# Mixture of experts in the order of their counts: second blocks on loaded weights, 64-row experts in pairs

## What is computed

```
gp = softmax(h @ w_rg + b_rg);  g_top, g_idx = top_k(gp, 1)
e_val, e_idx = top_k(el, 2)                       # two experts of the chosen group
expert = g_idx * 8 + e_idx
...
# expert e on its rows x: (silu(x @ w1[e]) * (x @ w3[e])) @ w2[e]
...
y = sum over the two of weights * y_expert
```

## Time and profile before

| | us |
|---|---|
| median of 3 runs | 2807.04 |
| lowest and highest run | 2804.06, 2811.59 |
| span of the profiled execution | 2805.2 |
| first matmul of the expert products (PE) | 674.40 |
| last matmul of the expert stage | 1250.21 |
| last matmul of the overflow stage | 1315.62 |
| first matmul of the next stage | 1329.25 |

### The profile page before, as it was taken

One profiled execution on the slowest core, in us unless ns is written; L12 is line 12 of the kernel. 1 busy time (PEld: TensorE's weight loads), 2 busy tenths in 40 slices (PEclk: granted clock), 3 DMA queues, 4 the chain that ended last, 5 costly groups with the idle time before them and its releaser, 6 DMA issues. The chain is left out here.

```text
span 2805.2 us, 34722 instructions
## 1 busy us (share of the span) xinstructions
PE 2696.0 (96%) x13265; PEld 2307.2 (82%) x13265; DVE 2087.0 (74%) x2831; ACT 1433.1 (51%) x1907; POOL 933.4 (33%) x493
## 2 busy tenths in 40 slices
PE   7999998996999999997988999999999999999999
PEld 4878886685888888876866899999999988888888
DVE  6376645556988888886664689788888778888883
ACT  4232124424777887766342334578878533333332
POOL 1425441231222222221222346533333434444420
PEclk9999999997999999998889999999999999999999
DMA  7336321115999999997310335689999999999992
GB/s 273 107 129 244 120 90 45 58 50 223 356 370 390 382 365 360 359 343 278 110 53 27 101 104 176 214 304 349 352 346 342 372 355 377 376 376 379 381 354 98
DMA packets 174282, 707.59 MB, mean 252 GB/s; under 512 B 24960, under 2 KB 52384, under 8 KB 140064
## 3 DMA queue, kind: packets, MB, share of 16 engines
q1 hardware_dynamic: 90864, 464.38, 45.2%
q0 software_dynamic: 47232, 142.66, 13.6%
q10 hardware_dynamic: 36016, 98.28, 9.3%
HBM read 661.70 MB, written 72.88 MB: 262 GB/s over the span
## 5 line engine op out<-in xcount | busy, mean ns | idle before, releaser
L2341 ACT ACTIVATE peer_high<-ring 128x1024 fp32r<-128x1024 f32 x268 | 283.1, 1056 | 318.9 <-PE psum L137 318.9
L2473 DVE TENSOR_TENSOR peer_low<-ring,peer_high 128x1024 fp32r<-128x1024 f32 x216 | 264.7, 1225 | 196.3 <-ACT peer_high L2341 191.9
L135 PE MATMUL psum<-h_high,peer_high 128*128 128x384 f32 (+1 forms) x1152 | 398.5, 346 | 3.2 <-DVE h_low L2623 3.2
L137 PE MATMUL psum<-h_high,peer_low 128*128 128x384 f32 (+1 forms) x1152 | 393.0, 341 | 0.0
L136 PE MATMUL psum<-h_low,peer_high 128*128 128x384 f32 (+1 forms) x1152 | 393.0, 341 | 0.0
L129 POOL TENSOR_TENSOR mx_slab_low<-mx_half_slab,mx_slab_high 128x1024 fp32r<-128x1024 f32 x85 | 215.1, 2533 | 397.2 <-ACT mx_slab_high L120 343.6
L1475 DVE TENSOR_TENSOR slab_low_moe<-half_slab_moe,slab_high_moe 128x2048 fp32r<-128x2048 f32 x126 | 285.6, 2288 | 52.0 <-ACT slab_high_moe L1417 51.9
L2226 POOL DMA_INDIRECT pe_rows<-in_v_rows,pe_place x128 | 202.5, 1582 | 251.3 <-DVE pe_sums L2595 215.8
L2226 POOL DMA_INDIRECT pe_rows<-in_u_rows,pe_place x128 | 167.9, 1312 | 282.7 <-DVE pe_row_act L2583 264.3
L1417 ACT ACTIVATE slab_high_moe<-half_slab_moe 128x2048 fp32r<-128x2048 f32 x126 | 234.0, 1908 | 24.9 <-issue 24.9
L135 PE MATMUL psum<-slab_high_moe,moe_x_high 128*128 128x512 f32 x560 | 224.4, 401 | 7.3 <-issue 3.7
(11 more groups left out here) (495 smaller groups left out, 6520.3 us busy)
## 6 DMA issues: line engine op xcount, KB each, us to landing
half_slab_moe<-in_weights SPq DMA_DIRECT2D x128, 1024.0 KB, 8.2
ring<-in_weights SPq DMA_DIRECT2D x162, 512.0 KB, 4.7
hT<-in_weights SPq DMA_DIRECT2D x64, 1024.0 KB
ring<-in_v_rows SPq DMA_DIRECT2D x128, 512.0 KB
mx_half_slab<-in_weights SPq DMA_DIRECT2D x44, 1024.0 KB, 5.1
gates_rows<-pe_table ACTq DMA_DIRECT2D x12, 2048.0 KB
pe_gt<-gates_rows ACTq DMA_DIRECT2D x16, 1536.0 KB
gelu_rows<-pe_gl ACTq DMA_DIRECT2D x30, 768.0 KB
```

What stands on the lines that cost most here:

```text
L135: pe.matmul(out, w[0], x[0], start=start, stop=False)
L137: return pe.matmul(out, w[1], x[0], start=False, stop=stop)
L2341: act.activation(high[:, g % RING, :], raw[:, g % RING, :], ACT.Copy).then_inc(highs, 1)
L2473: dve.tensor_tensor(low[:, g % RING, :], raw[:, g % RING, :], high[:, g % RING, :].bitcast(F32), ALU.subtract).then_inc(lows_dve, 1)
```

## The change

The blocks are laid out by rank. `stage_route` ranks the experts by their counts (expert 0 always comes first, as its first slabs are loaded before the route is known). Ranks 0 to 15 have a block of their own. Ranks 16 to 31 have at most 64 rows each (sixteen others have at least as many, and there are 1024 rows), and rank 16 + i shares a gathered block with rank 24 + i: slots 0 to 63 and 64 to 127. Ranks 1 to 3 get a second block, always. What goes beyond that still goes to the overflow stage, which now has 5 bodies and not 7. So there are 16 + 8 + 3 = 27 gathered blocks and 35 units of products: 13 of kind "whole", 3 "twice", 3 "again" (the second block of a "twice") and 16 "small".

The units run in the order: whole (rank 0), whole (4), small (16), small (24), twice (1), again (1), whole (5), small (17), small (25), twice (2), again (2), and so on. A small unit holds 64 columns of rows on PE and still streams 512 columns of weights. An "again" unit uses the slabs of its "twice" unit: they stay in their places for both, and its gate goes to bank 7, its down to banks 7 and 0. SP now takes the expert's number from `m.steer` for every expert but the first. The overflow stage loses its early start in the expert stage: the first load, gather and split of an overflow block move into `body`, and the last store of the expert stage moves out of it.

```diff
-OVER = 7
-BLOCKS = EXPERTS + OVER + 1
+OVER = 5
+SMALL = 64
+PAIRS = 8
+WHOLE = EXPERTS - 2 * PAIRS
+TWICE = 3
+C_AGAIN = WHOLE + PAIRS
+C_OVER = C_AGAIN + TWICE
+BLOCKS = C_OVER + OVER
...
+            chain(dve.scalar_tensor_tensor(out=key[:, :], in0=count, scalar=float(E), in1=less_number[:, :],
+                                           op0=ALU.mult, op1=ALU.add))
+            chain(dve.tensor_tensor(above[:, :, :], bcast(key[:, :], 1, E), bcast(key[:, :], 2, E), ALU.is_gt))
+            chain(dve.tensor_reduce(place_of[:, :], above[:, :, :], AX.X, ALU.add))
...
+            chain(dve.tensor_tensor(blocks_hot[:, :, :, :], bcast(flat_hot, 1, 4), bcast(blocks_of[:, :, :], 2, 2 * TT), ALU.mult))
+            chain(dve.tensor_reduce(blocks[:, :, :], blocks_hot[:, :, :, :], AX.X, ALU.add))
...
-            chain(dve.tensor_tensor(tmp[:, :, :, :], starts.unsqueeze(1).unsqueeze(1).to_broadcast([P, 2, TT, E]),
-                                    hot[:, :, :, :], ALU.mult))
-            chain(dve.tensor_reduce(ov[:, :, :], tmp[:, :, :, :], AX.X, ALU.add))
...
+            chain(dve.tensor_tensor(above[:, :, :], bcast(place_of[:, :], 1, E), bcast(iota[:, 0:E], 2, E), ALU.is_equal))
+            chain(dve.tensor_tensor(above[:, :, :], above[:, :, :], bcast(iota[:, 0:E], 1, E), ALU.mult))
+            chain(dve.tensor_reduce(at_place[:, :], above[:, :, :], AX.X, ALU.add))
+            chain(dve.tensor_copy(m.steer[:, 0:E], at_place[:, :]))
...
+def moe_units():
+    wholes = [0, 4, 1, 5, 2, 6, 3, 7] + list(range(8, WHOLE))
...
         @block.sync
...
+                if j >= 1 and w == 0:
+                    number[j] = sp.value_load(m.steer[0:1, places[j]:places[j] + 1], min_val=0, max_val=E - 1)
...
         @block.tensor
...
+                if units[u].kind == "twice":
+                    gate_half(u + 1, 0)
+                    gate_half(u + 1, 1)
+                    up(u)
+                    turn_x_of(u + 2)
+                    up(u + 1)
+                    gate_half(u + 2, 0)
+                    turn_hid(u)
+                    gate_half(u + 2, 1)
+                    turn_x_of(u + 3)
+                    down(u, range(2))
+                    turn_hid(u + 1)
+                    down(u, range(2, 4))
+                    down(u + 1)
...
         @block.vector
...
+                if units[u].kind == "twice":
+                    low(at_gate(units[u + 2].job), 0)
+                    hidden(u)
+                    low(at_gate(units[u + 2].job), 1)
+                    turned_of(u + 2)
+                    hidden(u + 1)
+                    low(at_down(units[u].job), 0)
+                    hidden_low(u)
+                    low(at_down(units[u].job), 1)
+                    low(at_up(units[u + 2].job), 0)
+                    low(at_up(units[u + 2].job), 1)
+                    turned_of(u + 3)
+                    hidden_low(u + 1)
```

621 lines of the change are left out of this document (356 added, 265 removed).

## The result

The changed kernel takes **2825.3 us** (median of 4 runs, 2820.9 to 2827.4), the kernel before 2806.1 beside it (4 runs, 2804.1 to 2811.6): a ratio of 1.0066, with a 95% interval from 1.0052 to 1.0080. The forecast was 2805.0, its range 2791 to 2819. The profiled execution of the changed kernel spans 2823.3 us, against 2805.2: 18.1 us more, with a mean granted clock of 0.970 of full speed against 0.976.

The account below looks back on a forecast made before the run. PE's own work was taken as the bound. Route +10.0, expert stage -13.1 and tail +1.0 sum to -2.1 us, so 2803.1 for the profiled execution and 2805 with 1.8 to the median; range 2791 to 2819.

Parts of the forecast that it names:

- The route, +10.0: Ahead of the first gather: added DVE steps delay `tokens` by 11.3 us, 1.3 of it hidden by the `h_rows` stores.
- The blocks: Expert stage: 35 units, with the three largest experts in ranks 1 to 3, so no overflow body runs.
- rival D: Overflow stage: one body still runs, adding 20.5 us and a half-clock start, about 2827 us; chance 0.02.
- The "twice" groups, 7.2: Expert stage: PE waits 2.4 us for the last `moe_hid_low` in each of three groups, 7.2 us together.
- the upper bound of 12.3: "Twice" groups: 4.1 us each if the clock falls for some nine matmuls behind the gap.
- The narrow units, 0: Small units on PE: 64 held columns keep the pace of 0.2267 us for a matmul, no difference.
- B: Rival on small units: 64 held columns make products cheaper, 15.4 us go, 2789.6 us; chance 0.08.
- C: Rival on PE: 107 passages between array shares each wait 0.16 us, costing 17.1 us, 2822 us; chance 0.09.
- -13.1: First to last expert or overflow matmul: 628.3 us against 641.4, with the groups' waits included.
- The tail, +1.0: Behind the experts: a second meeting, skipped bodies and ring loads cost between -2 and +3 us, taken as +1.0.
- all while the store is under way: Tail: the second meeting, the count's read and five skipped bodies pass during the last store.
- Rival E: Expert stage: another wait of the new order, up to 8 us and a little clock, up to 2816; slower part 0.10.

Follow-up runs that it names:

- all columns held: Changed kernel with the 16 small units holding all 128 columns of their gathered block and copying out only their own 64 rows: 2816.4 us, ratio 1.0036.
- the names late: Changed kernel with the four VectorE route steps that order the experts' names moved from ahead of the token list to behind the pairs list: 2822.5 us, ratio 1.0050.
- the last version: Changed kernel with ring loads early, overflow bodies nested, ScalarE and VectorE reordered in the "twice" groups, and small units holding 128 columns: 2799.5 us, ratio 0.9984.
- the nested form: Changed kernel with its five overflow bodies one inside another's condition, so one jump passes them all: 2822.6 us, ratio 1.0050, tail 16.4 us.

## Why the prediction was wrong

Point by point, by its own steps.

- **The route, +10.0: right.** The first matmul came 10.4 us later, 11.1 from the route's start on, which this profile reaches 0.7 us sooner. The count of DVE's steps and their prices held to 0.1 us; the store's hidden 1.3 us was right as well. The 0.8 us of a longer way through the gather and 0.3 of POOL's start were missing.
- **The blocks: right.** No row of `ov_hid` in the trace, three groups, 35 units; rival D did not come.
- **The "twice" groups, 7.2: the mechanism right, the size wrong by 4.6.** The wait of 2.4 was 2.05. But "nothing but one short gap is there" was the reason for leaving out the clock, and all three gaps were followed by eight to nine matmuls at half of it. Moving one step in two queues took away 11.8 us, near the upper bound of 12.3 that the forecast gave and didn't take. The row with which it weighed this, behind 3.9 us without work, pointed to that bound. That all three gaps were followed by the slow matmuls is partly luck: in the runs with all columns held and with the names late two and one of the same three were.
- **The narrow units, 0: wrong by 4.7.** "I take no difference" rested on eight matmuls of 128 streamed columns in the attention; with 512 streamed columns the pace is 0.2300 against 0.2267, which makes 3.8 of it. B's reasoning (a cheaper hold) had the wrong sign. C had the right sign, but its mechanism gives 0.9 us and not 17.1: only the way into the transposes of a narrow unit is longer, by 0.10 us, and the passages between 64 and 128 held columns aren't. The Trainium skill has the rule that a change of the tiling mode drains TensorE (TensorEngine Tiling (Array Packing), section Key Properties). The 0.33 against 0.23 us ahead of the narrow transposes agree with it, the 0.23 us between the products of 64 and 128 held columns show no drain, and no run isolates either.
- **The rest of the stage: 2.2 us missed.** The last unit's half clock takes 1.2. About 1.0 isn't laid out; it is in the last version too, whose stage of 621.8 is 0.9 above what the forecast gives without the groups' waits (641.2 - 13.1 - 7.2 = 620.9). Together -13.1 + 4.6 + 4.7 + 2.2 = -1.6.
- **The tail, +1.0: wrong by 5.3, and outside its own bounds of -2 to +3.** The step that failed is "all while the store is under way". The store doesn't cover the jumps: PE comes to the meeting 10.8 us behind the store's issue, POOL with the store landed 6.7 behind it. PE's third and fifth jump take 8.7 us, where the forecast had nothing. 4.6 us of the 6.3 hang on bodies that never run (3.5 by the nested form). The ring loads took 2.9. The forecast had left some 1.6 us for them (5.6 less 4), and at another place, in front of the loads of `y_rows`; they act on PE's jump.
- **Rival E** ("another wait, and a little clock") had 0.10 for the slower half and a price up to 2816. The time lies beyond it, because two more terms were off in the same direction.

The forecast failed by the sum of three terms, each taken at or near the cheap end of its bounds: 4.6 in the groups, 4.7 in the narrow units, 5.3 in the tail. The range was made from single rivals, and not from several terms going to their upper bounds together. That is why 2825 fell outside it.

## What to carry to other kernels

A change that takes some 20 us of work off PE (the stage of the last version is 19.5 shorter) can be eaten by things that don't compute: here 10 us on the one engine ahead of the first gather, 12 us by one step's place in two queues, 6 us by PE's jumps over code that isn't run and by loads issued beside them. When work disappears from the end of a stage, look at what it covered; ring loads and jumps were free only as long as overflow blocks ran beside them. And a wait "for PE's sequencer" is worth a look at that sequencer's own rows: they named two jumps out of five. And where a forecast has a wait on PE in an otherwise unbroken stream, add the clock to it: the gap and the slow matmuls behind it cost nearly the same here.

## What the runs showed of the hardware

- **The clock behind a short gap.** After 2.05 us without a matmul PE's granted clock fell to half for eight or nine matmuls, at a cost of 1.6 to 1.7 us, beginning 1.0 to 1.5 us after PE had started again. It fell behind all three such gaps in the changed kernel, behind two of three in the run with all columns held and behind one of three in the run with the names late, with the same gap at the same place in the program. What decides it isn't shown.
- **64 against 128 held columns.** With 512 streamed columns in this number format, a product with 64 held columns took 0.2300 us and one with 128 took 0.2267. Holding half as many columns was dearer by 1.5%. Between a product and the transposes of 64 rows behind it lie 0.33 us, ahead of those of 128 rows 0.23.
- **Jumps of PE over code that isn't run.** On ACT, DVE, POOL and SP each of five jumps took 0.04 to 0.07 us. On PE three took 0.22 to 0.44 and two 5.82 and 2.87; one far jump over all five bodies took 6.45, a single near one 0.25. Each long one had a 16 KB packet of the instruction queue in it and ended 1.3 to 1.4 us behind that packet's end.
- **Loads beside an instruction packet.** With four loads of 512 KB just issued, the packet of the first long jump started 3.48 us into it, without them 0.69 us; the jump took 5.82 and 3.16 us.
- **Loads beside a store.** The same loads, issued 0.75 us ahead of an indirect store in the kernel before, made it land 9.2 us after its issue instead of 3.9, and all that depends on it 5.4 us later. Issued together with the store, in the changed kernel, they put POOL's arrival at the meeting at 6.7 us instead of 2.4, with PE's jumps still the last.
